# Stick-breaking attention with queries on partitions: running sums on VectorE, weights transposed

## The reference

```python
z = einsum('bhtd,bhsd->bhts', q, k) * 64 ** -0.5
log_1m = where(s < t, log_sigmoid(-z), 0.0)
suffix = cumsum(log_1m, axis=keys, reverse=True) - log_1m
a = where(s < t, exp(log_sigmoid(z) + suffix), 0.0)
o = einsum('bhts,bhsd->bhtd', a, v)          # then o @ w_out
```

## Time and profile before

| what | value |
|---|---|
| median of three runs | 1318.77 us |
| profiled execution, its time | 1319.46 us |
| profiled execution, its span | 1317.7 us |
| mean granted TensorE clock | 0.997 of 2.4 GHz |
| first score group to first product after the stage's last wait | 462.6 to 561.0 us |

### The profile page before, as it was taken

The page is one execution under the profiler, slowest core; times in us unless marked ns, Lnnn a source line. Parts: engine busy times, 40 slices in busy tenths (PEclk is TensorE's granted clock), DMA queues, the critical chain, the costliest instruction groups (busy, mean ns, idle before and its releaser), DMA issues.

```text
span 1317.7 us, 17683 instructions
## 1 busy us (share of the span) xinstructions
PE 1296.9 (98%) x7329; PEld 1119.3 (85%) x7329; DVE 854.7 (65%) x995; ACT 707.7 (54%) x968; POOL 111.2 (8%) x177
## 2 busy tenths in 40 slices
PE   7999999999999999999999999999999999999999
PEld 6889897988888888889888888898877888788887
DVE  4556664776666744377576666668785566787775
ACT  4654544644444577865454444555556654645553
POOL 7200100100000100020100000101330003000000
PEclk9999999999999999999999999999999999899999
DMA  8753643555555444244255555553444445355552
GB/s 259 247 169 131 205 162 118 186 192 192 191 192 191 166 157 159 96 160 160 97 191 194 190 191 192 174 195 112 160 135 153 160 129 191 128 192 191 192 192 96
DMA packets 156113, 223.64 MB, mean 170 GB/s; under 512 B 6103, under 2 KB 107635, under 8 KB 156032
## 3 DMA queue, kind: packets, MB, share of 16 engines
q1 hardware_dynamic: 154240, 218.18, 49.4%
q0 software_dynamic: 1664, 4.27, 1.0%
q10 hardware_dynamic: 128, 0.05, 0.0%
HBM read 221.44 MB, written 1.05 MB: 169 GB/s over the span
## 4 chain that ended last, share of the span: by engine, by line
PE 92%; DVE 3%; ACT 2%; POOL 1%; issue 1%; DMA 1%; SPq 0%; POOLq 0%; ACTq 0%
PE ps L397 19%; PE ps L421 9%; PE ps L399 9%; PE ps L423 9%; PE ps L422 9%; PE ps L382 5%; PE ps L383 5%; PE ps L384 5%; PE ps L559 4%; PE ps L561 4%; PE ps L560 4%; DVE wlo L1564 1%; PE ps L853 1%; PE ps L446 1%; ACT whi L1062 1%; PE ps L494 1%
## 5 line engine op out<-in xcount | busy, mean ns | idle before, releaser
L1062 ACT ACTIVATE whi<-raw 128x1024 fp32r<-128x1024 f32 x412 | 426.1, 1053 | 356.2 <-PE ps L397 167.5
L1564 DVE TENSOR_TENSOR wlo<-raw,whi 128x1024 fp32r<-128x1024 f32 x411 | 494.0, 1231 | 188.0 <-ACT whi L1062 184.6
L397 PE MATMUL ps<-RR,whi 128*128 128x512 f32 x1056 | 366.3, 398 | 0.8 <-DVE RR L1594 0.8
L399 PE MATMUL ps<-RR,wlo 128*128 128x256 f32 x1056 | 274.2, 280 | 0.1
L421 PE MATMUL ps<-whi,RR 128*128 128x512 f32 x592 | 237.6, 401 | 3.7 <-DVE ar L1627 1.6
L423 PE MATMUL ps<-whi,RR 128*128 128x512 f32 x592 | 231.3, 391 | 0.0
L422 PE MATMUL ps<-wlo,RR 128*128 128x512 f32 x592 | 231.1, 390 | 0.0
L397 PEld LDWEIGHTS ps<-RR,whi 128*128 128x128 f32 x1056 | 191.8, 189 | 37.6 <-DVE wlo L1564 1.2
L399 PEld LDWEIGHTS ps<-RR,wlo 128*128 128x128 f32 x1056 | 200.2, 190 | 12.3 <-DVE RR L1594 0.4
L382 PE MATMUL ps<-RR,whi 128*128 128x256 f32 x512 | 147.3, 288 | 1.7 <-DVE RR L1594 1.3
L383 PE MATMUL ps<-RR,whi 128*128 128x256 f32 x512 | 145.5, 284 | 0.0
(11 more groups left out here) (333 smaller groups left out, 1267.5 us busy)
## 6 DMA issues: line engine op xcount, KB each, us to landing
raw<-in_ffn_w_gate_up SPq DMA_DIRECT2D x44, 1024.0 KB, 5.0
raw<-in_ffn_w_down SPq DMA_DIRECT2D x33, 1024.0 KB, 4.8
raw<-in_w_in SPq DMA_DIRECT2D x28, 1024.0 KB, 4.9
raw<-in_ffn_w_up SPq DMA_DIRECT2D x22, 1024.0 KB, 5.0
raw<-in_xa_w_kv SPq DMA_DIRECT2D x16, 1024.0 KB, 5.1
raw<-in_sb_w_qkv SPq DMA_DIRECT2D x12, 1024.0 KB, 5.1
raw<-in_ml_w_in SPq DMA_DIRECT2D x11, 1024.0 KB, 5.7
raw<-in_xa_w_q SPq DMA_DIRECT2D x8, 1024.0 KB, 5.1
```

The costliest lines, as they stand in the source:

```text
L397: m = pe.matmul(two(ps[:, bank, :]), p.hi[:, k, :], XT2[:, k, :, :], start=k == 0, stop=k == 7)
L399: pe.matmul(ps[:, bank, 0:256], p.lo[:, k, :], X.h[:, k, :], start=False, stop=False)
L1062: act.activation(p.hi, p.raw, ACT.Copy).then_inc(S["w_hi"], 1)
L1564: dve.tensor_tensor(p.lo, p.raw, p.hi.bitcast(F32), ALU.subtract).then_inc(S["w_lo"], 2 if p.n == 2 else 1)
```

## The change

Scores are made with queries on partitions: `qT` is the stationary operand and `kT` the moving one, and the masks change sides likewise. Of the 384 columns, the first 128 are query tile 0 by key tile 0, the other 256 query tile 1 by all keys. VectorE makes softplus as before, then for each head a running sum over the reversed row of 384, which a row `within` of ones with two zeros restarts between the query tiles, and then subtracts it from the scores (`sb_sums`). ScalarE's Exp works in place on `Sp` (`sb_exps`). TensorE turns the weights block by block, six transposes a pair, into the banks that held the scores (`sb_turn`), and VectorE copies them to `Aw` (`sb_turned`, semaphore `sb_c`). The value products are as they were. The scores of pair p wait for the copy of pair p - 2 instead of its Exp.

`sbk3` moves ahead of `sbv1`. The three lists are written out anew without the loop; `fm_piece` and `tm_piece` are the halves of `fm` and `tm_tile`, so that small groups can stand between the halves of a chunk, and the last output chunks `sbo2` and `sbo3` are taken in halves, alternately, around turn(7) and values(7). The last output pair goes to bank 4 instead of bank 3. `triN` and `onesN` are gone.

```diff
         for name, c in (("sbq0", 0), ("sbk0", 1024), ("sbq1", 256), ("sbk1", 1280)):
             chunk(name, W[:, c:c + 256], "c")
         tm_block("sbv0", W, 2048)
-        for name, c in (("sbq2", 512), ("sbk2", 1536), ("sbq3", 768)):
+        for name, c in (("sbq2", 512), ("sbk2", 1536), ("sbq3", 768), ("sbk3", 1792)):
             chunk(name, W[:, c:c + 256], "c")
         tm_block("sbv1", W, 2560)
-        chunk("sbk3", W[:, 1792:2048], "c")
         keys_chunk(1, 3)
...
+        within = reg(12672, 384)
...
             def fm(name, X, bank):
+                for i in range(2):
+                    fm_piece(name, X, bank, i)
+            def fm_piece(name, X, bank, i):
...
                 if not t:
                     m.then_inc(S["tm_first"], 1)
+            def tm_piece(name, X, k0, K, bank, t, i):
+                o, p = ps[:, bank, :], C[name].pieces[i]
...
             def sb_scores(p):
+                if p >= 2:
+                    pe.wait_ge(S["sb_c"], p - 1)
+                if p % 2 == 0:
+                    pe.wait_ge(S["sb_q"], p // 2 + 1)
+                    pe.wait_ge(S["sb_k"], p // 2 + 1)
                 both = [(ps[:, 4 + 2 * (p % 2) + h, :], slice(64 * h, 64 * h + 64)) for h in range(2)]
                 for o, r in both:
-                    pe.matmul(o[:, 0:128], identb[:, :], mStr[:, :], start=True, stop=False, skip_group_check=True)
-                    pe.matmul(o[:, 256:384], identb[:, :], mStr[:, :], start=False, stop=False, skip_group_check=True)
+                    pe.matmul(o[:, 0:128], mStr[:, :], identb[:, :], start=True, stop=False, skip_group_check=True)
+                    pe.matmul(o[:, 256:384], mStr[:, :], identb[:, :], start=False, stop=False, skip_group_check=True)
                 for o, r in both:
-                    m = pe.matmul(o[:, 0:256], kT[r, p, 0:128], qT[r, p, :], start=False, stop=False, skip_group_check=True)
+                    m = pe.matmul(o[:, 128:384], qT[r, p, 128:256], kT[r, p, :], start=False, stop=False, skip_group_check=True)
                 m.then_inc(S["sb_z"], 1)
                 for o, r in both:
-                    m = pe.matmul(o[:, 256:384], kT[r, p, 128:256], qT[r, p, 128:256], start=False, stop=False,
-                                  skip_group_check=True)
+                    m = pe.matmul(o[:, 0:128], qT[r, p, 0:128], kT[r, p, 0:128], start=False, stop=True, skip_group_check=True)
                     m.then_inc(S["sb_z"], 1)
-            def sb_weights(p):
-                pe.wait_ge(S["sb_sp"], p + 1)
+            def sb_turn(p):
+                pe.wait_ge(S["sb_a"], p + 1)
                 for h in range(2):
-                    o = ps[:, 4 + 2 * (p % 2) + h, :]
-                    s = Sp[p % 3][:, h, :]
-                    pe.matmul(o[:, 0:256], triN[:, :], s[:, 0:256], start=False, stop=False, skip_group_check=True)
-                    pe.matmul(o[:, 128:256], onesN[:, :], s[:, 256:384], start=False, stop=False, skip_group_check=True)
-                    m = pe.matmul(o[:, 256:384], triN[:, :], s[:, 256:384], start=False, stop=True, skip_group_check=True)
-                m.then_inc(S["sb_w"], 1)
+                    for j in range(3):
+                        c = slice(128 * j, 128 * j + 128)
+                        m = pe.transpose(ps[:, 4 + 2 * (p % 2) + h, c], Sp[p % 3][:, h, c], ident[:, :])
+                m.then_inc(S["sb_t"], 1)
             def sb_values(p):
                 c = 256 * (p % 2)
-                pe.wait_ge(S["sb_a"], p + 1)
+                pe.wait_ge(S["sb_c"], p + 1)
+                if p % 4 == 0:
+                    pe.wait_ge(S["sbv_dve"], p // 4 + 1)
+                    pe.wait_ge(S["sbv_act"], p // 4 + 1)
+                if p in (2, 4):
+                    pe.wait_ge(S["sb_lo"], p // 2)
                 for h in range(2):
-                    o = ps[64 * h:64 * h + 64, 3, :]
+                    o = ps[64 * h:64 * h + 64, 3 if p < 6 else 4, :]
                     d = 128 * p + 64 * h
                     pe.matmul(o[:, c:c + 256], Vs[:, 0, d:d + 64], Aw[p % 2][:, h, 0:256], start=True, stop=False,
                               skip_group_check=True)
...
                                   stop=True, skip_group_check=True)
                 m.then_inc(S["sb_v"], 1)
-            for i in range(10):
...
+            pe.wait_ge(X.sem, X.need[2])
+            fm("sbq0", X, 0)
+            fm("sbk0", X, 1)
+            fm("sbq1", X, 2)
+            pe.wait_ge(S["V_dve"], 3)
+            pe.wait_ge(S["V_act"], 3)
+            sb_scores(0)
+            fm("sbk1", X, 0)
+            tm_tile("sbv0a", X, 0, 8, 1, 0)
+            sb_scores(1)
+            pe.wait_ge(S["sb_q"], 2)
+            tm_tile("sbv0a", X, 0, 8, 2, 1)
+            tm_tile("sbv0b", X, 4, 8, 1, 0)
+            sb_turn(0)
+            tm_tile("sbv0b", X, 4, 8, 2, 1)
+            sb_scores(2)
+            fm("sbq2", X, 0)
+            sb_turn(1)
+            sb_values(0)
+            pe.wait_ge(S["sbv_dve"], 1)
+            fm_piece("sbk2", X, 1, 0)
+            sb_scores(3)
+            fm_piece("sbk2", X, 1, 1)
+            pe.wait_ge(S["sbv_act"], 1)
+            fm_piece("sbq3", X, 2, 0)
+            sb_turn(2)
+            sb_values(1)
+            fm_piece("sbq3", X, 2, 1)
+            sb_scores(4)
+            pe.wait_ge(S["sb_q"], 3)
+            fm("sbk3", X, 0)
+            sb_turn(3)
+            sb_values(2)
+            tm_tile("sbv1a", X, 0, 8, 1, 0)
+            sb_scores(5)
+            pe.wait_ge(S["sb_q"], 4)
+            tm_tile("sbv1a", X, 0, 8, 2, 1)
+            tm_tile("sbv1b", X, 4, 8, 1, 0)
+            sb_turn(4)
+            sb_values(3)
+            tm_tile("sbv1b", X, 4, 8, 2, 1)
+            sb_scores(6)
+            keys(1, 3, 0, M)
+            sb_turn(5)
+            sb_values(4)
+            sb_scores(7)
+            pe.wait_ge(S["K_act"], 4)
+            tm_tile("sbo0", sb_O, 0, 8, 0, 0)
+            sb_turn(6)
+            tm_tile("sbo0", sb_O, 0, 8, 2, 1)
+            sb_values(5)
+            tm_tile("sbo1", sb_O, 0, 8, 1, 0)
+            sb_values(6)
+            pe.wait_ge(S["sb_lo"], 3)
             tm_tile("sbo1", sb_O, 0, 8, 3, 1)
-            out_chunk("sbo", 2, sb_O)
-            out_chunk("sbo", 3, sb_O)
+            sb_turn(7)
+            tm_piece("sbo2", sb_O, 4, 8, 0, 0, 0)
+            tm_piece("sbo2", sb_O, 4, 8, 2, 1, 0).then_inc(S["w_used"], 1)
+            sb_values(7)
+            tm_piece("sbo3", sb_O, 4, 8, 1, 0, 0)
+            tm_piece("sbo3", sb_O, 4, 8, 3, 1, 0)
+            tm_piece("sbo2", sb_O, 4, 8, 0, 0, 1).then_inc(S["tm_first"], 1)
+            tm_piece("sbo2", sb_O, 4, 8, 2, 1, 1).then_inc(S["w_used"], 2)
+            tm_piece("sbo3", sb_O, 4, 8, 1, 0, 1).then_inc(S["tm_first"], 1)
+            tm_piece("sbo3", sb_O, 4, 8, 3, 1, 1).then_inc(S["w_used"], 1)
...
+            def sb_logs(p):
+                b, s = 4 + 2 * (p % 2), Sp[p % 3]
+                act.wait_ge(S["sb_z"], 3 * p + 3)
+                act.wait_ge(S["act_step"], step(act.activation(s, ps[:, b:b + 2, 0:384], ACT.Abs)))
+                act.wait_ge(S["act_step"], step(act.activation(s, s, ACT.Exp, scale=-1.0)))
+                act.activation(s, s, ACT.Ln, bias=1.0).then_inc(S["sb_ln"], 1)
+            def sb_exps(p):
+                act.wait_ge(S["sb_w"], p + 1)
+                act.activation(Sp[p % 3], Sp[p % 3], ACT.Exp).then_inc(S["sb_a"], 1)
+            def sb_out(n):
+                act.wait_ge(S["sb_v"], 2 * n + 2)
+                act.activation(Oh2[n], two(ps[:, 3 if n < 3 else 4, :]), ACT.Copy).then_inc(S["sb_hi"], 1)
+            sb_q(0)
+            past("sbk0")
+            sb_q(1)
+            sb_logs(0)
+            past("sbk1")
+            sb_exps(0)
+            sb_logs(1)
+            past("sbv0b")
+            evac(Vs[:, 1, 0:512], "sbv0b", 2, "sbv_act")
+            sb_exps(1)
+            sb_logs(2)
+            sb_q(2)
+            hi_to(end("sbk2") - 1 + NSP)
+            sb_exps(2)
+            sb_logs(3)
+            past("sbk2")
+            hi_to(end("sbq3") - 1 + NSP)
+            sb_out(0)
+            sb_q(3)
+            sb_exps(3)
+            sb_logs(4)
+            past("sbk3")
+            sb_exps(4)
+            sb_logs(5)
+            past("sbv1a")
+            sb_out(1)
+            past("sbv1b")
+            evac(Vs[:, 1, 512:1024], "sbv1b", 2, "sbv_act")
+            sb_exps(5)
+            sb_logs(6)
+            past("K1_3")
+            act.wait_ge(S["w_used"], end("K1_3"))
+            act.activation(Kx[:, 6:8, :], two(ps[:, 0, :]), ACT.Copy).then_inc(S["K_act"], 1)
+            sb_exps(6)
+            sb_logs(7)
+            past("sbo0")
+            sb_out(2)
+            sb_exps(7)
+            past("sbo1")
+            hi_to(end("sbo2") - 1 + NSP)
+            sb_out(3)
             past("sbo2")
...
-                    dve.tensor_tensor(Ol2[p], two(ps[:, 3, :]), Oh2[p].bitcast(F32), ALU.subtract).then_inc(S["sb_lo"], 1)
```

(67 more changed lines are left out.)

184 lines of the change are left out of this document (28 added, 156 removed).

## The result

The changed kernel takes 1332.85 us (median of 4 runs, 1332.01 to 1333.21), beside 1319.67 for the kernel before in the same comparison (1318.74 to 1320.74): a ratio of 1.010, 95% interval 1.0087 to 1.0112. It is 13 us slower. The forecast was 1320.5 and the range ended at 1325, so both missed. The profiled execution has a span of 1331.3, 13.6 more than before.

The account below looks back on a forecast made before the run. TensorE was taken as the bound: 11.2 us gained (work saved plus an end wait of 1.5), less 11.0 of new waits, plus 1.9 for low clock, gave 1321.2 profiled, 1320.5 us as median; range 1312 to 1325.

Parts of the forecast that it names:

- The work saved: TensorE, attention stage: 15.6 us of sum products go, 5.0 of transposes and 0.9 of restarts come in.
- I laid the queues of TensorE, ScalarE and VectorE side by side: Attention stage: the three engines' instruction lists compared at traced prices; new TensorE waits of 11.0 us in sum.
- Pairs 4 and 6 come out level, within 0.3: Scores of pairs 4 and 6: chains to the needed copy about as long as TensorE's work beside them, within 0.3 us.
- sbo1, V1_1b: After scores(7): TensorE waits 0.6 us for the third output remainder at sbo1's second tile, 0.7 for V1_1b's weight remainder.
- The waits forecast for scores(3), (5) and (7): Waits for copies of pairs 1, 3 and 5: 2.0 us (0.5 of it at scores(2)), 2.7 and 5.0.
- The chain worked out for scores(7): From the end of sbv1b's second tile to copy(5): 13.4 us, against 8.5 of TensorE work; wait 4.9, 5.0 used.
- I expect the same there: Behind the 5 us wait at scores(7): TensorE's clock falls to 1.2 GHz, as once in the earlier trace.
- the price of 1.9: Behind scores(7): 3.8 us of work at half rate loses 1.9 us, which nothing behind it can absorb.
- Clock falls twice: Rival: the clock falls at scores(5) too, 1.9 us more, 1322.4 us; chance 0.15.
- Reversed sums are slow: Rival: VectorE's reversed running sums take 1.9 us each, queues lose 8 more, about 1328 us; chance 0.08.
- The queues keep up: Rival: ScalarE and VectorE deliver copies in time, the whole 11.2 us gain comes through, 1307.6 us; chance 0.15 for some form.

Follow-up runs that it names:

- e8_list: Changed kernel with VectorE's list reordered: copies ahead of the next sums, each remainder where TensorE needs it next, key evictions no longer dragging remainders along; 1310.14 us.
- e4_fill: Changed kernel with unused short bf16 products on TensorE ahead of scores(2), (4), (6) and (7) to keep the clock up; 1328.17 us.
- e9_copy_then_remainders: Changed kernel with copies still behind the next pair's sums, remainders moved behind the copies (one still ahead of sums(5)), key evictions not dragging remainders; 1316.76 us.
- e5_copies_only: Changed kernel with each copy moved ahead of the next pair's sums, the remainders staying ahead of the sums; 1316.83 us.
- e1_sums_first: Changed kernel with the remainders ahead of sums(1), (2), (4), (5) and (6) moved behind those sums, copies left in place; 1327.95 us.
- e3_no_running_sums: Changed kernel without the two running sums of each pair, VectorE's list otherwise as changed, so the output differs; 1321.43 us.
- e6_no_turn: Changed kernel without the six transposes and the copy of each pair, Exp writing Aw directly, so value products multiply the wrong way round; 1311.77 us.
- e2_copies_first: Changed kernel with only VectorE's list reordered: copies ahead of the next sums, remainders later, no instruction added or left out; 1313.63 us.

## Why the prediction was wrong

**The bound.** Right: TensorE sets the time, and what matters is who makes it wait. VectorE's busy share is 66% in the changed kernel and 67% in e8_list, 22.7 us below it.

**The prices.** Mostly right. Reversed sums 0.946 (0.95 forecast). Six transposes take 0.57, 478.96 to 479.53, where a weight product follows (0.62 forecast), and 0.75 where the values follow, as in five of eight pairs. The switch of tables: a load of 1.28 and then the Ln 1.29 behind its start, as in the earlier trace rows, so the Trainium skill's 2.66 us ("ScalarE: Activation LUTs", "What ACT_TABLE_LOAD costs") isn't seen after the change either.

**The work saved.** Forecast 15.6 - 5.0 - 0.9 = 9.7; measured 119.05 - 110.91 = 8.1. From start to start, the turns are 5.5 in e8_list (five of 0.75, three of about 0.6) and the sum products were 15.3 (six of 1.95, one of 1.85, one of 1.78), so 15.3 - 5.5 - 8.1 = 1.7 is left for the restarts instead of 0.9. In sum a term that was 1.6 too large.

**The waits: the step that failed.** "I laid the queues of TensorE, ScalarE and VectorE side by side" gave 11.0 in the sum, and "Pairs 4 and 6 come out level, within 0.3". The laid-out queues had VectorE's remainders as work of 1.15 each, but not as waiting instructions: those ahead of sums(1), (2), (4), (5) and (6), and the one that `sb_k(2)` brings ahead of sums(3), need high parts that ScalarE makes only behind the logs of the same pair. So sums(p) start up to a wait and two remainders behind their Ln, instead of with it. What that made of each:

| TensorE waits at | forecast | changed kernel |
|---|---|---|
| scores(2) | 0.5 | 3.13 |
| scores(3) | 1.5 | 0.77 |
| scores(4) | level | 3.11 |
| scores(5) | 2.7 | 1.48 |
| scores(6) | level | 1.78 |
| scores(7) | 5.0 | 3.83 |
| sbo1, V1_1b | 0.6, 0.7 | 0.28, 0.41 |

The waits forecast for scores(3), (5) and (7) are there and shorter; those at (2), (4) and (6) make 8.0 in place of 0.5. The two are linked, as I read it: a late pair 2 makes TensorE late, and the others then catch up for pair 3. The chain worked out for scores(7) has the gap too: it lets sums(6) start with Ln(6), and it started 2.5 later. At full clock the sum is 17.1 to 18.7 (e4_fill) in place of 11.0, so 6.1 to 7.7 short. e9_copy_then_remainders shows the cause from the other side: with the remainders that pair p brings behind copy(p - 1), and the copies still behind the sums, the waits at scores(2) and scores(4) are gone, those for the copies are 4.9 in all, and the kernel takes 1316.8.

**The clock.** "I expect the same there" was right for scores(7), and there the price of 1.9 was right as well: the low clock lasted some 3.6 us, and e9_copy_then_remainders with one such fall worked 112.79 - 110.91 = 1.9 us longer. That nothing can absorb it was not quite so, since filling that wait brought 1.4 to 1.5. Wrong were the count and the length. The clock fell behind scores(2), (4), (6) and (7), since the waits left out above were long, and the first two falls lasted 5.8 and 6.7 us. The work took 9.0 us longer, more than four times 1.9; net it is 5.1 to 6.7 by e4_fill, not 1.9. The 3.8 us that the price was taken from are only the end of a longer low stretch in the trace of before, which had begun before the last short wait, so that the price fitted scores(7) in part by luck:

```profile
1127.00:1133.50 6.50, 5.72 (x20) 4.87 (x21) 5.44 (x10) 3.30 (x8) 0.00 (x0) 0.50 0.48 161
```

**The sum.** By the stretches the forecast is 120.48 - 0.2 + 1.9 = 122.2 and the changed kernel's is 134.7, 12.5 more: 1.6 of work, 6.1 to 7.7 of waits and 3.2 to 4.8 of the clock beyond the 1.9, where a larger share of the waits goes with a smaller one of the clock. By the times it is 1332.85 - 1320.5 = 12.35.

**The rivals.** *Clock falls twice* and *Reversed sums are slow* were the two ways to a slower kernel, and neither had the mechanism; the sums were at their forecast price. The prediction was to be wrong if the low clock cost over 4 us, and it did; its other two signs, waits for the copies below 6 us and a running sum over 1.1, didn't come. That the work saved shows on TensorE once the waits are gone (e8_list, some 9 us faster) is what *The queues keep up* said, though with the changed kernel's list it is not so.

**What stays open.** Why either move alone brings 16 us (e5_copies_only against the changed kernel, and e9_copy_then_remainders) and both 22.7 is argued and not shown pair by pair: copy(p - 1) is late by the wait for the high parts, the remainders and the sums, one behind the other, and either move takes a part of that chain away from it, the sums in e5_copies_only and the remainders in e9_copy_then_remainders. For pair 0 the traces show it: copy(0) starts 18.5 and 19.0 us behind the first score product there, and 22.2 in the changed kernel. And e1_sums_first, which moved most but not all of the remainders, brought only 4.9; the traces show the rest at scores(2) and scores(4), but no run takes each away by itself. How much of the low clock comes back as shorter waits is known only within the range above.

## What to carry to other kernels

When an engine gets new duties, write down for each instruction in its list not only its length but what it waits for, helpers that hide instructions (`sb_k` begins with `past`) included: the new work was there in full in the kernel that was 9 us faster than before (e8_list); what cost was instructions that stood idle ahead of work that was ready. Put what frees a buffer for the bound engine (the copy) ahead of the next item's long chain, and background work behind it. And before giving up a change that takes work off the bound engine but is slower, count its waits: reordering one list turned +13 us into -9.

## What the runs showed of the hardware

The granted clock of TensorE behind a wait, over the profiles of this stage: it stayed at 1.00, that is 2.4 GHz, behind all waits up to 1.48 us, among them 1.43 before, 1.44 in e3_no_running_sums and 0.77 and 1.48 in the changed kernel. It went to 0.50, 1.2 GHz, for some 3 to 7 us behind those of 1.78, 3.11, 3.13 and 3.83 in the changed kernel, 1.70 and 2.89 in e6_no_turn, 1.97 in e2_copies_first, 2.12 in e4_fill, 2.17, 4.04 and 5.00 in e1_sums_first, 4.98 in e3_no_running_sums, 2.72 in e5_copies_only and 2.89 in e9_copy_then_remainders. I had expected it only for the longest. The length of one wait doesn't settle it, though. Behind 2.63 at scores(7) in e4_fill, with the 50 short products just ahead of that wait, it stayed at 1.00; and in the trace of before it fell at about 1126.9, behind waits of 1.45 and 0.84 close together. The windows of the changed kernel behind the waits of 0.77 and 1.48:

```profile
500.60:504.00 3.40, 3.38 (x30) 3.11 (x31) 1.23 (x1) 3.34 (x5) 0.00 (x0) 1.00 0.90 281
...
531.40:535.00 3.60, 3.56 (x22) 2.90 (x23) 0.00 (x0) 2.19 (x3) 0.00 (x0) 1.00 0.76 284
```

Short bfloat16 products in the idle time kept it up where they stood, and a low clock costs less than the rows at half rate say, when other engines are behind: in the changed kernel 9.0 us longer work, 5.1 to 6.7 us net.

A running sum costs more for each column than the other passes: two of 384 columns take from 481.92 to 483.76, 1.84, where softplus over the same 768 columns takes 0.98 (480.94 to 481.92), a factor of 1.9. The Trainium skill ("DVE: opcode table, instruction layouts, handler registers and perf-mode slots", "6. Datapath and trigger behaviour") says that this instruction's program runs at half throughput; the trace agrees. The reversed direction costs nothing that shows: 0.946 beside the 0.95 that the forward rows give for 384 columns.
